# Sums of squares behind the experts: squares as the weights of products with one column, two sum banks, no turned row of roots

## The reference, cut to what matters

```python
x = x + g2 * expert_choice_ffn(hx2, w_router, w_gate, w_up, w_down)
...
def rmsnorm_2(x, g):
    xf = x.astype(jnp.float32)
    y = xf * lax.rsqrt(jnp.mean(xf * xf, axis=-1, keepdims=True) + EPS)
    return (y * g.astype(jnp.float32)).astype(x.dtype)
...
def even_layer(x, norm_g, w_in, pool_w, pool_scale, ws, bs, w_out):
    h = rmsnorm_2(x, norm_g)
    z = h @ w_in
```

## Time and profile before

| | us |
|---|---|
| median of 3 runs | 3382.1 |
| lowest and highest of them | 3379.6, 3382.46 |
| the profiled execution | 3379.95 |
| its span | 3377.9 |
| TensorE busy | 3125.4 (93%) |
| weight loads of TensorE busy | 2573.3 (76%) |
| VectorE busy | 1851.4 (55%) |
| GpSimd busy | 1611.9 (48%) |
| ScalarE busy | 1269.4 (38%) |

### The profile page before, as it was taken

One profiled execution on the slowest core, in us unless ns is written; L12 is line 12 of the kernel. 1 busy time (PEld: TensorE's weight loads), 2 busy tenths in 40 slices (PEclk: granted clock), 3 DMA queues, 4 the chain that ended last, 5 costly groups with the idle time before them and its releaser, 6 DMA issues. The chain is left out here.

```text
span 3377.9 us, 43503 instructions
## 1 busy us (share of the span) xinstructions
PE 3125.4 (93%) x15972; PEld 2573.3 (76%) x15972; DVE 1851.4 (55%) x2678; ACT 1269.4 (38%) x2146; POOL 1611.9 (48%) x1056
## 2 busy tenths in 40 slices
PE   4979997969599969999999799999999999999999
PEld 3767786757388837778888588888888888888887
DVE  5566223662699856544361665555556556555712
ACT  5256122741477732222220343443344444222311
POOL 2331231123312217777743465565566556688732
PEclk8989998979799979999999899999999999999999
DMA  8230112035599961222251111111111111222331
GB/s 291 47 88 21 49 43 78 28 105 195 187 378 396 395 193 54 74 67 81 72 187 64 50 48 47 54 51 44 48 48 51 50 41 54 82 63 81 110 106 69
DMA packets 312571, 353.89 MB, mean 105 GB/s; under 512 B 28488, under 2 KB 280300, under 8 KB 306101
## 3 DMA queue, kind: packets, MB, share of 16 engines
q1 hardware_dynamic: 301182, 311.36, 27.5%
q0 software_dynamic: 4608, 16.78, 2.0%
q10 hardware_dynamic: 6582, 23.13, 1.7%
HBM read 293.28 MB, written 54.53 MB: 103 GB/s over the span
## 5 line engine op out<-in xcount | busy, mean ns | idle before, releaser
L2584 POOL TENSOR_TENSOR odd_quarter_lo<-odd_w_sums,odd_quarter_hi 128x512 fp32r<-128x512 f32 x224 | 300.3, 1342 | 278.2 <-ACT odd_quarter_hi L2579 276.7
L2619 PE MATMUL first_z<-odd_t_hi,odd_quarter_hi 128*128 128x512 f32 x784 | 327.5, 418 | 18.1 <-DVE odd_t_lo L4073 18.1
L2619 PE MATMUL odd_z<-odd_t_hi,odd_quarter_hi 128*128 128x512 f32 x784 | 325.5, 415 | 1.1 <-POOL odd_quarter_lo L2584 1.1
L2584 POOL TENSOR_TENSOR odd_quarter_lo<-odd_raw,odd_quarter_hi 128x512 fp32r<-128x512 f32 x168 | 232.0, 1381 | 167.4 <-ACT odd_quarter_hi L2579 163.0
L2621 PE MATMUL first_z<-odd_t_hi,odd_quarter_lo 128*128 128x512 f32 x784 | 308.3, 393 | 0.0
L2620 PE MATMUL first_z<-odd_t_lo,odd_quarter_hi 128*128 128x512 f32 x784 | 307.1, 392 | 0.0
L2621 PE MATMUL odd_z<-odd_t_hi,odd_quarter_lo 128*128 128x512 f32 x784 | 307.0, 392 | 0.0
L2620 PE MATMUL odd_z<-odd_t_lo,odd_quarter_hi 128*128 128x512 f32 x784 | 305.5, 390 | 0.0
L2579 ACT CAST odd_quarter_hi<-odd_w_sums 128x512 fp32r<-128x512 f32 x224 | 139.7, 624 | 365.6 <-PE odd_z L2621 178.8
L2635 DVE SCALAR_TENSOR_TENSOR dil_set<-first_z,dil_set 128x512 f32<-128x512 f32 x196 | 170.6, 884 | 143.3 <-PE first_z L2621 138.8
L2635 DVE SCALAR_TENSOR_TENSOR dil_set<-odd_z,dil_set 128x512 f32<-128x512 f32 x196 | 170.7, 884 | 138.4 <-PE odd_z L2621 133.5
(11 more groups left out here) (602 smaller groups left out, 8213.8 us busy)
## 6 DMA issues: line engine op xcount, KB each, us to landing
odd_raw<-in_odd_w_in SPq DMA_DIRECT2D x224, 256.0 KB, 3.1
raw_gate<-in_w_gate SPq DMA_DIRECT2D x16, 2048.0 KB, 15.0
raw_up<-in_w_up SPq DMA_DIRECT2D x16, 2048.0 KB, 14.8
raw_down<-in_w_down SPq DMA_DIRECT2D x16, 2048.0 KB, 15.2
even_raw<-in_even_w_in SPq DMA_DIRECT2D x80, 256.0 KB, 3.3
start_w_mod<-in_w_mod SPq DMA_DIRECT2D x11, 1024.0 KB, 10.8
w_raw<-in_w_in SPq DMA_DIRECT2D x16, 512.0 KB, 5.2
scan_w_mod<-in_w_mod SPq DMA_DIRECT2D x8, 1024.0 KB, 11.2
```

The costliest lines, as they stand in the source:

```text
L2584: pool.tensor_tensor(self.w_lo[:, n % self.SLOTS], self.source(m, i), self.w_hi[:, n % self.SLOTS].bitcast(F32), ALU.subtract).then_inc(se ...
L2619: pe.matmul(to, self.w_hi[:, slot, kt], t_hi[:, kt], start=(kt == 0), stop=False)
```

## The change

The squares become the weights. For each half `a` of a group (128 tokens) 8 products accumulate with a 128x128 tile of squares as weights and the column of ones moving. The sums come out as a column for each half, tokens on the partitions, so no row has to be turned: the root reads the two columns and writes them to `roots` in SBUF, and VectorE inverts these. `turn_root` and its semaphore are gone. The sums of neighbouring groups go to the two banks of `aux` in turn; from the third group on, `sum_up` waits until the root two groups earlier was taken. In TensorE's list `sum_up(g + 1)` now stands ahead of `spread_out(g)`, and one wait for all roots stands ahead of the next use of `aux`.

```diff
-            root_rows = root_mem("even_root_rows", [1, 2, T])
+            roots = root_mem("even_roots", [P, BLOCKS])
...
-            root_turned = sem("even_root_turned")
...
-                norm_sums = aux[:, 0, :]
                 spread = [acc[:, u, 0:T] for u in range(2)]
+
+                def norm_sums(g):
+                    return aux[:, g % 2, 2 * g:2 * g + 2]
...
                     def sum_up(g):
                         pe.wait_ge(sq_done, g + 1)
-                        for kt in range(KT):
-                            ins = pe.matmul(norm_sums[0:1, 0:T], ones[:, 0:1], sq[:, g % 2, kt, :], start=(kt == 0), stop=(kt == KT - 1))
+                        if g >= 2:
+                            pe.wait_ge(root_done, g - 1)
+                        for a in range(2):
+                            for kt in range(KT):
+                                ins = pe.matmul(norm_sums(g)[:, a:a + 1], sq[:, g % 2, kt, a * P:(a + 1) * P], ones[:, 0:1], start=(kt == 0), stop=(kt == KT - 1))
                         ins.then_inc(summed, 1)
-
-                    def turn_root(g):
-                        pe.wait_ge(root_done, g + 1)
-                        for a in range(2):
-                            ins = pe.transpose(norm_sums[:, T + 2 * g + a:T + 2 * g + a + 1], root_rows[:, g % 2, a * P:(a + 1) * P], ident[0:1, 0:1])
-                        ins.then_inc(root_turned, 1)
...
                     turn_rows(2)
                     sum_up(0)
                     turn_rows(3)
-                    turn_root(0)
+                    sum_up(1)
                     spread_out(0)
-                    sum_up(1)
-                    turn_root(1)
+                    sum_up(2)
                     spread_out(1)
-                    sum_up(2)
-                    turn_root(2)
+                    sum_up(3)
                     spread_out(2)
-                    sum_up(3)
-                    turn_root(3)
                     spread_out(3)
+                    pe.wait_ge(root_done, GROUPS)
                     pe.wait_ge(masked, 1)
...
                     def root(g):
                         act.wait_ge(summed, g + 1)
-                        if g >= 2:
-                            act.wait_ge(root_turned, g - 1)
-                        act.activation(root_rows[:, g % 2, :], norm_sums[0:1, 0:T], ACT.Sqrt, scale=1.0 / D, bias=eps_col[0:1, 0:1]).then_inc(root_done, 1)
+                        act.activation(roots[:, 2 * g:2 * g + 2], norm_sums(g), ACT.Sqrt, scale=1.0 / D, bias=eps_col[:, 0:1]).then_inc(root_done, 1)
...
                     def invert(g):
-                        dve.wait_ge(root_turned, g + 1)
-                        dve.reciprocal(rstd[:, 2 * g:2 * g + 2], norm_sums[:, T + 2 * g:T + 2 * g + 2]).then_inc(inverse_done, 1)
+                        dve.wait_ge(root_done, g + 1)
+                        dve.reciprocal(rstd[:, 2 * g:2 * g + 2], roots[:, 2 * g:2 * g + 2]).then_inc(inverse_done, 1)
```

## The result

| | us |
|---|---|
| median after (7 runs, 3386.28 to 3394.11) | 3391.1 |
| median before (7 runs beside it, 3379.6 to 3384.76) | 3381.24 |
| ratio, with its 95% interval | 1.0024 (1.0014 to 1.0034) |
| profiled execution after, and its span | 3386.58, 3384.5 |
| profiled execution before, and its span | 3379.95, 3377.9 |

The change costs 9.9 us of median, between 4.7 and 11.5 by the interval, where 8.3 were forecast. The recorded ratio isn't that of the medians (1.0029): the seven times of each kernel lie up to 8 us apart, and their means, 3389.8 and 3381.5, differ by 8.3. The profiled pair differs by 6.6 us of span.

What follows compares the result with a forecast made beforehand. TensorE, busy for 93% of the span, was taken as the bound, with VectorE setting the hand-over. A 9.4 us delay less 1.1 gave 8.3, added to 3382.1: 3390.4 us, range 3384.5 to 3395.5.

Steps and rivals of the forecast that it cites:

- first step: Hand-over behind the experts: VectorE's finish sets the stage, TensorE carries on from there, and the shift passes in full to the end.
- walk: Clock followed through sums and turnings, fall after 2.9 us, rise after 2.7: VectorE through at 1263.0, 9.4 us later.
- Rival D: After the norm: the delay arises but is taken up later, at most 6 us left, about 3384 to 3388; chance 0.07.
- Part 1: Norm: the turned row leaves the ring, sums run beside scalings at 3.84 us a group; the first spread comes late.
- Rival C: Norm sums: one-column products hold the high clock; +0.1 - 1.1 = -1.0 us, 3381.1; chance 0.12.
- Part 2: Norm sums: a group's 32 records cost 3.76 us at the high clock or 6.82 low, against 3.61 before.
- Part 3: Norm: weight loads with few moving columns lose TensorE's high clock, turnings lift it; VectorE through 9.4 us later.
- rival A: Norm: clock falls in one-column runs and returns in turnings, total 3390.4 us; chance 0.72.
- good side: Sum 0 and turnings stay high, two low sums follow, VectorE through at 1260.9: +6.2 us, 3388.3.
- Rival B: Norm: the clock does not come back during turn_rows(3); +12.1 - 1.1 = 11.0 us, 3393.1; chance 0.09.
- Part 4: First token sum behind the norm: GpSimd's addition of weights no longer meets VectorE's work, gaining 1.1 us.

Runs made afterwards that it cites:

- best of both: Kernel before with 128 columns of ones moving over squares as weights, no turned row, two casts ahead of root(3): ratio 0.9991, on another chip 0.9992.
- shape alone: Kernel after with TensorE's list back to sum and spread of the same group: median 3389.02 us against 3380.96, ratio 1.0028.
- half the dose: Kernel after with 128 moving columns for groups 0 and 1, one for groups 2 and 3: median 3381.12 us, ratio 1.0001.
- casts-first kernel: Kernel before with the third and fourth cast of weights ahead of root(3) on ScalarE: median 3380.97 us, ratio 0.9997.

## Why the prediction was right, and where not

**VectorE's pace sets the seam, and the shift passes to the end (first step): right, nearly in full.** VectorE's last scaling, TensorE's next set of products and GpSimd's next remainders all moved with the norm. TensorE is full again (9.76 of 9.80 us) from 1293.9 instead of 1288.2, 5.7 later; I had 1296.5, for the longer walk. Rival D, a delay taken up later, is out: VectorE is still 5.5 us later at 3169 (3163.43 before, 3168.97 after). But the 6.6 us of the two spans are not all of the change, as the issue of the last eight stores shows (timelines of SyncE, before and after):

```profile
3365.74 9.07 SPq L3668 DMA_DIRECT2D out<-last_rows  x8
```

```profile
3370.77 10.89 SPq L3661 DMA_DIRECT2D out<-last_rows  x8
```

It starts only 5.0 us later and lasts 1.8 us longer (SPq is SyncE's own sequencer). But one kernel has either length: 10.89, 10.73 and 9.04 us in the three profiles of the change, 9.06 and 10.89 in the two of the best of both. So the longer issue goes with the execution and not with the change, and the 1.6 us between 5.0 and 6.6 say nothing of the change; why it is longer no experiment asked. The first products behind the norm did stay longer at the low clock (the first twelve of the second set take 5.3 us, 1274.44 to 1279.72, against 4.4). Ahead of 1288.24 TensorE waited 0.75 us for GpSimd's remainder, ahead of 1293.94 only 0.34: GpSimd sets the pace at that point, and the 0 I gave to the longer low clock did no harm.

**Part 1, the new order costs a late first spread: right, and small.** With the old products it costs 1.3 us; with the short ring and the clock held, the norm is 0.7 shorter than before in spite of it. Rival C put the norm at +0.1. The root on 128 partitions takes 0.26 us instead of 0.47.

**Part 2, the price of 32 records: right.** I had 3.76 us high and 6.82 low; measured are 3.63 and 6.83.

**Part 3, the clock: the mechanism right, its sizes off, and the course not one but two.** That few moving columns lose the clock is shown by the kernel with 128 of them, where all else is the same. The step that was mis-sized is the fall "2.9 us into a run of one-column records": counted from the first such record it came after 3.9 us (first profile, by then in the turnings behind sum 0), 2.6 (second), 3.0 (third), 3.7 (shape alone) and 4.3 (half the dose). A single number stood for something that varies by 1.7 us from one execution to the next, and the 3.6 us of a sum lie in the middle of that. The rise was mis-sized too: 2.7 us into turnings in the walk, 3.8 us behind the first turning in the first profile (1231.71 to 1235.5, by then in the first records of sum 1) and 3.7 in the shape alone (1234.87 to 1238.5). So sums 0 and 1 took 3.63 and 4.01 us, nearly all at the high clock, where the walk has 4.4 for each, and VectorE was through at 1260.6 instead of 1263.0. That is the end of rival A's good side (1260.9), but not its course: it kept the turnings high and lost the clock late in sum 1, while here the turnings were low and sum 1 was high. Sum 1 was over at 1238.8 against 1238.6, two errors that cancel. That execution's time, 3386.58, lies near the 3388.3 of that side less the 2.15 us between the profiled execution and the median, and 1.6 us of it come with the longer issue of the stores.

**Rival B had too small a chance.** I gave it 0.09. In two of three profiles of the changed kernel the clock didn't come back behind the turnings of turn_rows(3), and the norm took 11.5 and 11.8 us more; B had 12.1. What I held against it, that 16 turnings last longer than the 2.7 us of 873.6, rested on one rise in the trace, while the other one I quoted, from 1220.0, needed 4.5 us. Two rises so different were a reason for a chance near even, and the second was the usual one: in the eleven profiles the turnings that open this stretch had run for 4.0 to 5.5 us when the clock rose, longer than the 3.5 that 16 of them last. In the four profiles with one-column products ahead of turn_rows(3) (three of the change, one of the shape alone) it was two against two: the clock came back where it had fallen late (3.9 and 3.7 us), and not where it had fallen early (2.6 and 3.0). Four profiles show no more than that; what decides it stays open. The Trainium skill (TensorE: Matmul & The Clock Gate, Part 4: PE-mode transpose) says that transposes don't count as activity for the clock. The traces agree with it in the second and third profile and disagree in the first and in the shape alone, where the clock rose right behind sixteen turnings, at 1235.5 and 1238.5, and in all eleven at the start of the stretch, where nothing but turnings had run since a pause of over 15 us.

So the median of 3391.1, 0.7 us from the forecast, does not confirm the walk as it stands: that it came so near is luck in part. The walk describes an execution between the two courses that were seen, and the seven runs lie on both sides of it: three within 0.3 us of 3386.3, four from 3391.1 to 3394.1. Which of the unprofiled runs took which course isn't known. The right text would have had two cases of like weight, near 3386 and 3391 for the profiled execution's own scale, with the same centre. The seams of the three profiles, 5.8, 10.2 and 9.8 us longer than before, have a mean of 8.6, where the walk has 8.3.

**Rival C is out**, and with it the reading that pauses alone cost the clock: there was none in the 25.50 us at 0.50. The Trainium skill (same page, HAM oscillation) ties the low clock to pauses between bursts; so here the clock was lost in another way than that.

**Part 4, the collision goes: right, 1.6 us instead of 1.1.** I counted the token sum (3.37 to 2.28) and left out the remainder ahead of it, which also shrinks, from 2.82 to 2.28, as rows 3 could have told; the casts-first kernel shows both. GpSimd was done 1.4 us ahead of VectorE's remainder (1257.93 + 1.26 against 1260.57), where I had 1.1. The collision is between VectorE and GpSimd: side by side the addition takes 3.33 us and the token sum 3.37, apart 1.26 and 2.28. The Trainium skill (SBUF — State Buffer, Who interferes with whom) says that a VectorE instruction with two inputs in SBUF contends with a GpSimd instruction that reads SBUF; the rows agree, and also in that GpSimd's addition beside VectorE's scalings, which have one input in PSUM, keeps its 1.26 us.

## What to carry to other kernels

Before a product is turned around so that the data are the weights and a single column moves, count its weight loads and ask what else holds TensorE's clock in that stretch: a busy engine was not enough here, and at half the clock the sums took 6.8 us instead of 3.6. If the turned form is wanted for its output (here a column for each token instead of a row), let more columns move, as many as the load hides: 128 instead of one cost 0.1 us in 3.7 and kept the clock. Nothing between 1 and 128 was measured here. And where a forecast rests on a clock that falls or rises within a stretch as long as the delay itself, take it as two courses with a chance each, and profile the kernel more than once before one trace is believed.

## What the runs showed of the hardware that I had not expected

- The same program takes different courses in one and the same stretch: sum 1 had 4.01 us in one execution and 6.83 in two others.
- From the first product of one column the high clock lasted 2.6 to 4.3 us in five executions, though TensorE was busy up to the fall (2.50 of 2.50 and 4.20 of 4.20 us in two of them).
- Behind a load of 128 weight columns, 32 records with 128 moving columns take 3.74 us and with one column 3.63, at the high clock both: the columns hardly count beside the load.
- A root of 128x2 elements out of PSUM takes 0.26 us, one of 1x256 0.47.
